# Moving half of a big operand tensor by 224 bytes in SBUF: x's rows brought to the same remainder of 512 bytes as the split weights

## The reference

```
h  = rmsnorm(x) * (1 + scale) + shift            # first block, modulated by c
u, q, k, v = h @ w_in ; the same for ctx
x += gate * rmsnorm(concat(pool_mixer(u), attention(q, k, v, k_ctx, v_ctx)) @ w_out)
x += gate * rmsnorm(square(relu(h2 @ w_mlp_in)) @ w_mlp_out)          # 4096 inner columns
x += 0.5 * (silu(n @ w_gate) * (n @ w_up)) @ w_down                    # second block, 2816 inner columns
x += concat(attention_a, attention_b)(n @ w_in_2) @ w_out_2
x += 0.5 * (silu(n @ w_gate2) * (n @ w_up2)) @ w_down2 ; x = rmsnorm(x)
```

## Time and profile before

| | |
|---|---|
| median of 3 executions | 828.15 us (828.08 to 828.53) |
| the profiled execution, its own time | 827.97 us |
| its span, first to last instruction | 826.1 us |
| granted TensorE clock over the span | 0.998 |
| PE busy | 805.8 us (98%) |
| DVE, ACT, POOL busy | 555.8, 468.2, 45.3 us |
| L1502 and L1504 (X moving) | 864 products each |
| L1529, L1531, L1533 (T stationary) | 500 products each |

### The profile page before, as it was taken

The page is one execution under the profiler, slowest core; times in us unless marked ns, Lnnn a source line. Parts: engine busy times, 40 slices in busy tenths (PEclk is TensorE's granted clock), DMA queues, the critical chain, the costliest instruction groups (busy, mean ns, idle before and its releaser), DMA issues.

```text
span 826.1 us, 12099 instructions
## 1 busy us (share of the span) xinstructions
PE 805.8 (98%) x4426; PEld 665.6 (81%) x4426; DVE 555.8 (67%) x971; ACT 468.2 (57%) x885; POOL 45.3 (5%) x63
## 2 busy tenths in 40 slices
PE   5999999899999999999999999999999999999996
PEld 2798767688888888788888888887677888888885
DVE  2389675778777676677666665597676676666652
ACT  4582576665445554566555554675776665555542
POOL 1010000100000000100000000059000000000000
PEclk9999999999999999999999999999999999999999
DMA  9997871349877655077666655184123386666501
GB/s 359 409 391 267 354 282 58 122 155 364 280 260 226 222 180 173 26 256 253 205 205 203 204 166 167 49 349 157 52 77 129 127 280 208 204 201 206 175 1 52
DMA packets 45243, 166.28 MB, mean 201 GB/s; under 512 B 4992, under 2 KB 5120, under 8 KB 44928
## 3 DMA queue, kind: packets, MB, share of 16 engines
q1 hardware_dynamic: 44896, 164.98, 58.5%
q10 hardware_dynamic: 288, 0.52, 0.2%
HBM read 164.43 MB, written 1.05 MB: 200 GB/s over the span
## 4 chain that ended last, share of the span: by engine, by line
PE 77%; ACT 2%; issue 1%; DVE 1%; POOL 0%; POOLq 0%; ACTq 0%; DVEq 0%
PE ps L1502 24%; PE ps L1504 13%; PE ps L1529 12%; PE ps L1531 11%; PE ps L1533 11%; PE ps L1729 1%; PE ps L1773 1%; PE ps L1812 1%; PE ps L1754 1%; ACT PT L538 1%; PE ps L1978 0%; PE ps L1731 0%; PE ps L1522 0%; PE ps L1524 0%; PE ps L1523 0%
## 5 line engine op out<-in xcount | busy, mean ns | idle before, releaser
L979 DVE TENSOR_TENSOR lo<-raw,hi 128x1024 fp32r<-128x1024 f32 (+2 forms) x247 | 293.7, 1217 | 98.3 <-ACT hi L526 98.2
L1502 PE MATMUL ps<-T,hi 128*128 128x512 f32 x864 | 303.7, 392 | 0.0
L526 ACT ACTIVATE hi<-raw 128x1024 fp32r<-128x1024 f32 (+2 forms) x247 | 249.6, 1044 | 15.4 <-DMA raw<-in_w_in_v 6.8
L1504 PE MATMUL ps<-T,lo 128*128 128x256 f32 x864 | 243.5, 282 | 0.0
L1502 PEld LDWEIGHTS ps<-T,hi 128*128 128x128 f32 x864 | 162.2, 188 | 35.1
L1529 PE MATMUL ps<-hi,T 128*128 128x512 f32 (+2 forms) x500 | 169.4, 396 | 0.4 <-DVE T L1218 0.4
L1531 PE MATMUL ps<-lo,T 128*128 128x512 f32 (+2 forms) x500 | 165.7, 389 | 0.0
L1533 PE MATMUL ps<-hi,T 128*128 128x512 f32 (+2 forms) x500 | 165.5, 389 | 0.0
L1504 PEld LDWEIGHTS ps<-T,lo 128*128 128x128 f32 x864 | 163.1, 189 | 2.4
L1533 PEld LDWEIGHTS ps<-hi,T 128*128 128x128 f32 x500 | 93.8, 188 | 19.8
L1531 PEld LDWEIGHTS ps<-lo,T 128*128 128x128 f32 x500 | 93.9, 188 | 19.2
(11 more groups left out here) (221 smaller groups left out, 757.9 us busy)
## 6 DMA issues: line engine op xcount, KB each, us to landing
raw<-in_ffn_down SPq DMA_DIRECT2D x44, 512.0 KB, 3.7
raw<-in_ffn_gate SPq DMA_DIRECT2D x40, 512.0 KB, 4.2
raw<-in_ffn_up SPq DMA_DIRECT2D x40, 512.0 KB, 4.0
raw<-in_w_mlp_out SPq DMA_DIRECT2D x32, 512.0 KB, 4.5
raw<-in_w_mlp_in SPq DMA_DIRECT2D x28, 512.0 KB, 4.3
raw<-in_w_mod_p SPq DMA_DIRECT2D x24, 512.0 KB, 6.6
raw<-in_w_mod_c SPq DMA_DIRECT2D x16, 512.0 KB, 5.9
raw<-in_w_out SPq DMA_DIRECT2D x16, 512.0 KB, 4.8
```

The lines of the kernel that those rows point to most:

```text
L526: e.activation(HI[SLOT[h]][:, 0:w], raw[n % RAW][:, 0:w], ACT.Copy).then_inc(s_hi, 1)
L979: e.tensor_tensor(LO[SLOT[h]][:, 0:w], raw[n % RAW][:, 0:w], HI[SLOT[h]][:, 0:w], ALU.subtract).then_inc(s_lo, 1)
L1502: e.matmul(o, a[:, k * P:(k + 1) * P], X[:, k].rearrange("p s w -> p (s w)"), start=(k == 0), stop=(k == KT - 1), skip_group_check=True)
L1504: m = e.matmul(o[:, 0:L], b[:, k * P:(k + 1) * P], Xh[:, k, :], start=False, stop=(k == KT - 1), skip_group_check=True)
```

## The change

Two numbers change: the gap of 56 floats between `X` and `Hd` is taken out, and the padding behind `cols` grows by the same 56 floats.

```diff
-        cols = sb("cols", [P, NCOLS + 16])[:, 0:NCOLS]
+        cols = sb("cols", [P, NCOLS + 72])[:, 0:NCOLS]
...
-        HD = 4096 + 56
+        HD = 4096
```

## The result

The changed kernel takes **831.3 us** (median of 6, 831.1 to 832.0) against 828.0 us of the kernel before (median of 6 on the same chip): a ratio of 1.0041, 95% interval 1.0031 to 1.0051. It is slower by 3.3 us, where 2.9 us less were forecast. The profiled execution took 831.98 us.

The account below looks back on a forecast made before the run. TensorE was taken as the bound, busy 805.8 of 826.1 us. Six items summed to 2.9 us saved: profiled 827.97 became 825.1, plus 0.2 for the median, 825.3 us; range 821.8 to 831.8, forecast's own 822.8 to 826.4.

Parts of the forecast that it names:

- Which operand is ahead of which matters too: Pairs with X moving 288 bytes away cost 13.3 ns extra a product, as from Hd, so distance alone isn't the rule.
- item 5: Switches between product kinds in 60 MLP blocks: half of 2.2 us saved, 1.1; nothing if width or load kind costs.
- 1, outside w_in_v: 512 column products from X, T stationary, in boundaries and w_in2: 190 of 288 save 6.5 ns each, 1.24 us.
- 1, w_in_v: Eight dozens of w_in_v products, X and Hd in turn: each dozen from 2.76 to 2.72 us, 0.3 us saved.
- 2, 416 columns: 48 products of 416 columns from X: an estimated 3 ns saved each, 0.1 us.
- 3, k: k's 96 products of 512 columns out of X and Hd: 6 ns less each from 232.8, 0.55 us saved.
- 4, u and q: 192 products of 256 columns in u and q: from 116.7 to 120 ns, partly hidden for u, 0.4 us lost.
- 6, 864 pairs: Pairs of 512 and 256 columns, X moving: 346.7 against 346.6 ns, 0; bounds 2.7 us saved to 5.8 lost.
- The pairs turn slow: Rival: at zero distance each pair loses 6.7 ns, 5.8 us over 864 pairs, giving 831.1 us; chance 0.27.

Follow-up runs that it names:

- run 4: Kernel before, with Hd as well as X put 288 bytes past the weights' remainder: 833.2 us, ratio 1.0067.
- Run 3: Kernel before, with wstat_both making its eight 512 column products first, then its eight 256 column ones: 832.8 us, one execution.
- Runs 1 and 2: Changed kernel, eight 512 column products before eight 256 column ones in wstat_both: 826.1 us; changed kernel, second product of every pair 512 columns too: 917.1 us.
- run 5: X put 32, 64, 128, 224 or 256 bytes past the weights' remainder, Hd at it: 828.3, 830.6, 831.3, 829.9, 831.2 us.
- run 6: Changed kernel with wstat_both's 512 column products grouped before its 256 column ones, except narrow first in the up weights' tile: 825.6 us.

## Why the prediction was wrong, by its own steps

**What bounds the kernel: right.** The added time is in the starts of TensorE's products. That the place of the stationary operand against the moving one has a price was right and is shown by moving it: X's products went from 233.3 to 226.7, and Hd's the other way in run 4. Identical instructions at other addresses made 3.3 us of difference. The Trainium skill's two independent read ports (TensorE: Matmul & The Clock Gate, Step-by-step: what each phase is for) were taken in the prediction to mean that no address matters; that conclusion does not hold here, though the page speaks of bandwidth and says nothing of addresses. What inside TensorE or SBUF makes the difference was not tried.

**One reading of the kernel before: wrong.** "Which operand is ahead of which matters too" was drawn from the pairs at 288. Run 3 shows 233.8 ns for the same wide products as soon as they stand in a uniform row, and 224 bytes, the other direction, runs as 32 does. What set the pairs apart from X's other products was the alternation of widths.

The terms of the prediction's sum, and what the two traces show for each as distances between starts (us gained; item 5 is what remains of the pairs and the products from Hd behind them when each is charged its settled price):

| | forecast | measured |
|---|---|---|
| 1, outside w_in_v | 1.24 | 1.06 |
| 1, w_in_v | 0.3 | 0.33 |
| 2, 416 columns | 0.1 | 0.02 |
| 3, k | 0.55 | 0.50 |
| 4, u and q | -0.4 | -0.44 |
| 5, switches | 1.1 | 0.5 |
| 6, 864 pairs | 0 | -5.8 |
| sum | 2.9 | -3.8 |

The two profiled executions are 4.0 us apart.

**Items 1, 3 and 4: right in price.** w_in2_q 10.93 us as forecast (10.9); w_in_v 2.72; k 226.7 for 226.7; q 120.0 for 120. Item 2 gave nothing worth naming: the 48 products of 416 columns take 9.59 us for 9.61. The first ahead products of the second boundary turned their gain into wait, 0.12 us for the 0.1 named.

**Item 6, the 864 pairs: the step that failed.** It took the middle of its bounds, 0, because "both widths known at equal remainder give" 346.7. The settled pair costs 353.3, and 864 x 6.7 = 5.8 us is the upper bound that the item itself gave. The rows it rested on, 512 columns and 384 columns, were uniform rows. Runs 1 and 2 show that the two prices are right for uniform rows at zero distance, and that their sum is wrong for rows in which the widths alternate: group the products, or make them equally wide, and the price is there.

The kernel before had two warnings. The first is the rule of adding itself: at 288 the uniform rows cost 233.3 and 116.7, 350.0 together, and the pair costs 346.6. A pair was never the sum of its two uniform rows. The table of run 5 says the same at every place, with a sign that changes: alternation saves 2 to 5 ns a pair at 32, 64, 128, 224 and 288, and costs 6.6 at 0 and 256. (This takes the price of a product with X stationary for one with X moving; run 3 bears that out at 288, and no run does elsewhere but 0.) The second is in the start of the very stretch of the earlier trace rows:

```profile
548.93 0.51 PE L1529 MATMUL ps<-hi,T 128*128 128x384 f32 x2
...
550.00 0.51 PE L1529 MATMUL ps<-hi,T 128*128 128x384 f32 x2
```

Six products right behind a row of 512 column ones take 1.07 us, 178 ns each, where the settled ones take 173.3. In the changed kernel, where no distance changes at that point, the same six take 1.07 us too, so it is not the distance. The prediction used the settled part and left out the unsettled one. In a pair the width changes with each product, so that an extra of this kind could be paid again and again; this fits the pairs at zero distance and is not shown further. Why alternation saves time at the other places, the runs don't say.

**Item 5, the switches: mis-sized.** It forecast half of 2.2 us back. Charged at settled prices (346.6 and 353.3 a pair, 226.8 a product from Hd), the pairs and the products from Hd behind them had 2.2 us on top before and have 1.7 in the changed kernel: 0.5 back. It came from the feed-forward layers, where a block of 16 pairs and twelve products had 33 ns on top and has 14. In the MLP's blocks of eight pairs nothing came back, and the extra rose by some 10 ns. There the pairs behind down products start fast (eight take 288.35 - 285.54 = 2.81 us, less than 8 x 353.3), but the twelve down products behind them take 2.78 us, where they took 2.74. Part of the item's own alternative was true: some of the cost is the change of width, which a place can't take away and run 6 did.

**The rival.** "The pairs turn slow" gave 831.1 us and 0.27; the time is 831.3. Its price for a settled pair (6.7) was right. That the total fits to 0.2 us is in part luck: it kept all of the other items' gains, 2.9 us, of which 2.0 came. Charged by where the time stands and not by settled prices, the 864 pairs lost 3.6 us together, 4.2 ns each, and the products from Hd behind them 1.7 us. Its mechanism, that the narrow product sets the loads at other points of time, is in accord with runs 1 and 2, but the runs show only that the alternation of widths is needed, not how it acts.

## What to carry to other kernels

When TensorE is the bound, measure a product by the distance between starts, and measure it in the very sequence of widths in which it will run: a price from a uniform row is not the price in an alternating one. The place of an operand in SBUF and the order of the products have to be chosen together; here, with the weights left where they were, uniform groups of 512 columns want both operands at the same remainder of 256 bytes, and alternating widths want them 32 bytes apart. Changing only one of the two loses, 3.3 us by place alone and 4.7 by order alone (one execution); changing both gains 1.9, and with fewer changes of width 2.5.

## What the runs showed of the hardware that was not expected

- The same float32r product of 512 columns at the granted clock of 2.4 GHz is spaced 226.7 or 233.3 ns in uniform rows by addresses alone, and one of 256 columns 116.7 or 120.0, with values between at 64 and 224. The better place for the one is the worse for the other.
- The pattern in the address repeats every 256 bytes at the places tried (0 like 256, 32 like 288), not every 512 as the change had it, and not every 128. Only `T` was moved; moving the weights was not tried.
- Alternating 512 and 256 columns costs 6.6 ns a pair over the uniform rows at equal remainder, and 2 to 5 less at the other five places, if a uniform row costs the same with either operand stationary (seen at 288 alone of the five).
- Behind a change from 256 to 512 columns TensorE needs some five products to settle, about 27 ns at equal remainder; the change back returns 7.
